# Modulation moved from the first attention (TensorE products) to the second (VectorE sums), context norm moved and done token by token

## The reference

```python
mod = jax.nn.silu(c) @ w_ada[l] + b_ada[l]
mod_c = jax.nn.silu(c_ctx) @ w_ada[l] + b_ada[l]
sh1, sc1, g1, sh2, sc2, g2 = jnp.split(mod[:, None, :], 6, axis=-1)
sh1c, sc1c, g1c, sh2c, sc2c, g2c = jnp.split(mod_c, 6)
mixed = _mixer(_modulate(ctx, sh1c, sc1c), _modulate(x, sh1, sc1), rows, w_in[l], ...)
```

## Time and profile before

| | |
|---|---|
| runs, us | 3023.42, 3021.66, 3011.48 (median 3021.66) |
| the profiled execution | 3016.62, its span 3014.8 |
| busy share of the span | PE 94%, PEld 76%, DVE 61%, ACT 42%, POOL 26% |
| chain that ended last, largest shares | PE 13%, DMA 4%, DVE 4% |
| DMA | 440.91 MB, mean 146 GB/s |

### The profile page before, as it was taken

One profiled execution on the slowest core, in us unless ns is written; L12 is line 12 of the kernel. 1 busy time (PEld: TensorE's weight loads), 2 busy tenths in 40 slices (PEclk: granted clock), 3 DMA queues, 4 the chain that ended last, 5 costly groups with the idle time before them and its releaser, 6 DMA issues. The chain is left out here.

```text
span 3014.8 us, 54412 instructions
## 1 busy us (share of the span) xinstructions
PE 2834.1 (94%) x22525; PEld 2295.6 (76%) x22525; DVE 1838.3 (61%) x2584; ACT 1272.0 (42%) x1629; POOL 796.9 (26%) x427
## 2 busy tenths in 40 slices
PE   9889999999999999999999999878989799999994
PEld 7467888889777777888867887567885478888883
DVE  3757663210343445655237967766656699999997
ACT  3544332222333334333226331423332277777775
POOL 2013444434333312444420000010000125544431
PEclk9999999999999999999999999889999799999997
DMA  4632422232211112222222200231003499999996
GB/s 173 236 142 112 98 97 98 98 131 96 84 58 69 71 57 84 98 97 97 98 99 98 84 23 12 102 142 46 32 18 124 161 333 363 370 372 368 379 368 260
DMA packets 83394, 440.91 MB, mean 146 GB/s; under 512 B 19712, under 2 KB 22784, under 8 KB 34816
## 3 DMA queue, kind: packets, MB, share of 16 engines
q1 hardware_dynamic: 73920, 429.63, 38.9%
q0 software_dynamic: 9280, 8.43, 0.8%
HBM read 423.30 MB, written 37.77 MB: 153 GB/s over the span
## 5 line engine op out<-in xcount | busy, mean ns | idle before, releaser
L85 POOL TENSOR_TENSOR ring_lo<-ring,unit_hi 128x2048 fp32r<-128x2048 f32 x110 | 507.3, 4612 | 1034.4 <-ACT unit_hi L74 1034.4
L146 PE MATMUL wide<-h_hi,unit_hi 128*128 128x512 f32 x1296 | 516.1, 398 | 11.7 <-DVE h_lo L623 5.0
L148 PE MATMUL wide<-h_hi,ring_lo 128*128 128x512 f32 x1296 | 507.0, 391 | 0.0
L147 PE MATMUL wide<-h_lo,unit_hi 128*128 128x512 f32 x1296 | 506.2, 391 | 0.0
L3479 DVE TENSOR_TENSOR ex_w_lo<-ring,ex_w_hi 128x2048 fp32r<-128x2048 f32 x194 | 442.1, 2290 | 41.6 <-ACT ex_w_hi L3474 40.8
L3474 ACT CAST ex_w_hi<-ring 128x2048 fp32r<-128x2048 f32 x194 | 369.5, 1908 | 111.5 <-DMA ring<-in_weights 99.3
L74 ACT CAST unit_hi<-ring 128x2048 fp32r<-128x2048 f32 x114 | 217.6, 1908 | 375.0 <-PE wide L148 370.8
L146 PEld LDWEIGHTS wide<-h_hi,unit_hi 128*128 128x128 f32 x1296 | 244.0, 188 | 71.4 <-issue 11.3
L148 PEld LDWEIGHTS wide<-h_hi,ring_lo 128*128 128x128 f32 x1296 | 244.1, 188 | 52.2
L147 PEld LDWEIGHTS wide<-h_lo,unit_hi 128*128 128x128 f32 x1296 | 244.4, 189 | 49.2 <-issue 0.7
L431 DVE TENSOR_TENSOR ffn_hidden_lo<-ffn_whole,ffn_hidden_hi 128x512 f32 (+1 forms) x44 | 201.3, 4575 | 51.9 <-ACT ffn_hidden_hi L402 51.9
(11 more groups left out here) (573 smaller groups left out, 5686.1 us busy)
## 6 DMA issues: line engine op xcount, KB each, us to landing
ring<-in_weights SPq DMA_DIRECT2D x356, 1024.0 KB, 6.2
rw_F<-factors SPq DMA_DIRECT2D x9, 1024.0 KB, 5.9
factors<-rp_out SPq DMA_DIRECT2D x4, 1280.0 KB, 5.3
factors<-rp_out SPq DMA_DIRECT2D x4, 1024.0 KB, 4.8
ex_both<-pair_rows_out SPq DMA_DIRECT2D x4, 1024.0 KB, 7.9
x<-in_x SPq DMA_DIRECT2D x8, 256.0 KB, 7.1
x_kept<-x SPq DMA_DIRECT2D x1, 2048.0 KB, 14.3
x<-x_kept SPq DMA_DIRECT2D x1, 2048.0 KB, 7.8
```

The source lines that it names most:

```text
L85: pool.tensor_tensor(self.lo[n % RING][:, :], self.ring[n % RING][:, :], self.hi[n % 2][:, :].bitcast(F32), ALU.subtract).then_inc(self.lo ...
L146: pe.matmul(dst, a[0], b[0], start=start, stop=False)
L147: pe.matmul(dst, a[0], b[1], start=False, stop=False)
L148: return pe.matmul(dst, a[1], b[0], start=False, stop=stop)
```

## The change

**Modulation.** It leaves attention A and the ring. `w_ada` is stored transposed, [48 x 128 outputs, 1024], and attention B computes each output as a sum along a row: one `tensor_tensor_reduce` on VectorE multiplies a chunk of 128 outputs x 512 inputs with half a row of silu(c) that stands in all partitions, and adds it up. There are 128 such sums (48 + 48 for `c`, 16 + 16 for `c_ctx`), each with a load of its own (256 KB) into one of two buffers; SyncE issues a load when the sum before last has released the buffer. silu of the conditions is taken in `v_b` on ScalarE, stored to HBM and loaded again spread over the partitions. Ring loads in attention B are now issued by ScalarE behind `write_hi` (`refill`), since SyncE's list holds the modulation's loads. The sums stand in VectorE's list: two behind each copy of a chunk of pair 0 but the first, then 6 in an item with two chunks and 3 in one with one chunk. `finish` (six small operations) stands in item 30.

**Context norm.** It moves from `out_a` to `out_b`, and works on tokens: two loads (512 KB each), `bn_stats`/`bn_aggr` on VectorE, a root on ScalarE, one normalising operation per 128 tokens, then four groups of four transposes on TensorE, after output chunks 1, 2, 3 and 5, whose results ScalarE scales, shifts and splits. Stores of the parts go to `out_b`, the four small stores of `mod_rows` from feed-forward 0 to 1.

```diff
@@ Weights
+    def refill(self, sp, i):
+        n = self.at + i
+        sp.wait_ge(self.used, n + 1)
+        sp.dma_start(self.ring[n % RING][:, :], self.stream[n + RING]).then_inc(self.loaded[n % RING], 16)
@@ ContextNorm
+    def moments(self, dve):
+        dve.wait_ge(self.loaded, 16 * (CTX // P))
+        for j in range(CTX // P):
+            for i in range(2):
+                dve.bn_stats(self.parts_of[:, j, i, :], self.rows[:, j, i * T:(i + 1) * T]).then_inc(self.step, 1)
...
+    def normalise(self, dve):
...
+        for j in range(CTX // P):
+            dve.tensor_scalar(self.rows[:, j, :], self.rows[:, j, :], self.stats[:, j, 0:1], self.rstd[:, j:j + 1],
+                              ALU.subtract, ALU.mult).then_inc(self.normed, 1)
...
+    def turn(self, pe, n):
+        if n == 0:
+            pe.wait_ge(self.normed, CTX // P)
+        else:
+            pe.wait_ge(self.placed, 2 * n)
...
@@ out_stage
+                if context:
+                    context.load(sp)
...
-                    context.square(act)
+                    context.root(act)
                 w.write_hi(act, 0, 2)
+                if context:
+                    context.place(act, 0)
+                    context.place(act, 1)
                 w.write_hi(act, 0, 3)
...
+                    if context and m_ in (3, 6):
+                        context.place(act, m_ // 3 + 1)
...
-                    if context and m_ == 0:
-                        context.tensor_sums(pe)
-                    if context and m_ == 3:
-                        context.tensor_squares(pe)
+                    if context and m_ in (1, 2, 3, 5):
+                        context.turn(pe, (1, 2, 3, 5).index(m_))
...
+                    if context and m_ in (0, 1, 4, 6):
+                        context.low(dve, (0, 1, 4, 6).index(m_))
@@ Modulation
+    DEEP, WIDE = 2, D // 2
...
+        for n, (f, m) in enumerate(self.steps):
+            if n >= self.DEEP:
+                sp.wait_ge(self.summed, n - self.DEEP + 1)
+            sp.dma_start(self.chunk[:, n % self.DEEP, :], self.ada[m, :, f % 2 * self.WIDE:(f % 2 + 1) * self.WIDE]).then_inc(self.loaded[n % self.DEEP], 16)
...
+    def vector(self, dve, n):
+        f, m = self.steps[n]
+        if m == 0:
+            dve.wait_ge(self.row_loaded[f % 2], 16 * (f // 2 + 1))
+        dve.wait_ge(self.loaded[n % self.DEEP], 16 * (n // self.DEEP + 1))
+        chunk, to = self.chunk[:, n % self.DEEP, :], (self.mod if f < 2 else self.mod1)
+        dve.tensor_tensor_reduce(chunk, chunk, self.rows[f % 2][:, :], 1.0, 0.0, ALU.mult, ALU.add, to[:, m, f % 2:f % 2 + 1]).then_inc(self.summed, 1)
@@ attention_stage, TensorE
-                    if modulation:
-                        for n in modulation.units_at(i, N):
-                            modulation.tensor(pe, n)
...
-                if modulation:
-                    modulation.add_strips(pe)
@@ attention_stage, VectorE
                 for j in range(per):
                     project.copy(dve, w, 0, j, pair_chunk_done, pair_chunk_copied)
+                    if j >= 1:
+                        sums(2)
...
+                    if chunks:
+                        sums(1)
...
+                    if len(chunks) == 1:
+                        sums(1)
...
+                        sums(2)
...
+                    if chunks:
+                        sums(1)
...
+                    if len(chunks) == 2:
+                        sums(2)
+                    if modulation and i == N - 2:
+                        assert next(summed, None) is None
+                        modulation.finish(dve)
@@ attention_stage, ScalarE
+                def write_hi(n):
+                    w.write_hi(act, 0, n)
+                    if n >= 2:
+                        w.refill(act, n - 2)
@@ values_b_stage
+                modulation.load_cond(sp, cond)
                 w.feed(sp, U_V_B)
+                modulation.store_cond(sp, cond)
...
                 normed.root(act)
+                modulation.silu(act, cond)
```

More of the change, by code:

```diff
@@ L492, in center @@
[L492 to L501, removed]
+        sp.dma_start(self.kept[1], self.parts[1][:, :, :].bitcast(F32)).then_inc(self.stored, 16)
@@ L509, in low @@
-    def low(self, dve):
-        for k in range(DC):
+        for j in range(CTX // P):
+            dve.tensor_scalar(self.rows[:, j, :], self.rows[:, j, :], self.stats[:, j, 0:1], self.rstd[:, j:j + 1],
[5 more added lines that the diff above has]
+            pe.wait_ge(self.placed, 2 * n)
+        for k in (2 * n, 2 * n + 1):
+            for j in range(CTX // P):
+                at = k % 2 * CTX + j * P
+                m = pe.transpose(self.c.bank[7][:, at:at + P], self.rows[:, j, k * P:(k + 1) * P], self.c.ident[:, :])
+        m.then_inc(self.turned, 1)
@@ new lines, in place, with low @@
+    def place(self, act, n):
+        act.wait_ge(self.turned, n + 1)
+        for k in (2 * n, 2 * n + 1):
+            act.activation(self.src[:, k, :], self.c.bank[7][:, k % 2 * CTX:(k % 2 + 1) * CTX], ACT.Identity,
+                           bias=self.shift(k), scale=self.scale(k)).then_inc(self.placed, 1)
+        for k in (2 * n, 2 * n + 1):
+            act.wait_ge(self.placed, k + 1)
+            act.copy(self.parts[0][:, k, :], self.src[:, k, :]).then_inc(self.hi_ready, 1)
+    def low(self, dve, n):
+        for k in (2 * n, 2 * n + 1):
@@ L523, in place @@
[L523 to L528, removed]
-        self.high(act, DC - 1)
-    def high(self, act, k):
-        act.wait_ge(self.placed, k + 1)
-        act.copy(self.parts[0][:, k, :], self.src[:, k, :]).then_inc(self.hi_ready, 1)
@@ L767, in sb, with load_cond, silu, store_cond @@
+    def load_cond(self, sp, room):
+        sp.dma_start(room, self.cond).then_inc(self.cond_loaded, 16)
+    def silu(self, act, room):
+        act.wait_ge(self.cond_loaded, 16)
+        act.activation(room, room, ACT.Silu).then_inc(self.cond_ready, 1)
+    def store_cond(self, sp, room):
+        sp.wait_ge(self.cond_ready, 1)
+        sp.dma_start(self.kept, room).then_inc(self.cond_stored, 16)
+    def place(self, ctx, nc):
         def sb(n, shape):
             return ctx.enter_context(nc.sbuf_tensor(f"ada_{n}", shape, F32))
-        self.c, self.w, self.cond, self.bias, self.mod, self.mod1 = c, w, cond, bias, mod, mod1
@@ L784, in tensor @@
-    def tensor(self, pe, n):
-        if n == 0:
-            pe.wait_ge(self.spread_ready, 1)
-        if n % 2 == 0 and n >= 2:
-            pe.wait_ge(self.rows_turned, n // 2)
-        unit = self.w.arrived(pe, 0, n)
-        for q in range(ADA_TILES):
-            m = pe.matmul(self.c.bank[7][q * ADA_WIDE:(q + 1) * ADA_WIDE, :], self.spread[:, n % 2 * ADA_TILES + q, :], unit[:, q * T:(q + 1) * T],
-                          start=(n % 2 == 0), stop=(n % 2 == 1))
-        m.then_inc(self.w.used, 1)
@@ L903, in _ @@
                 def _(sp):
-                    w.feed(sp, U_ADA)
+                    modulation.load(sp)
             if project:
@@ L1095, in _ @@
                                 write_due(due)
-    w.end(project.units if project else U_ADA, 1)
+                if project:
+                    for n in range(project.units - 2, project.units):
+                        w.refill(act, n)
+    w.end(project.units if project else 0, 1)
 def slopes():
```

205 lines of the change are left out of this document (90 added, 115 removed).

## The result

The changed kernel takes 3057.85 us (median of 3050.89, 3053.97, 3061.74 and 3061.88), the kernel before 3020.81 in the same comparison. The ratio is 1.0118, interval 1.0101 to 1.0135: slower by 1.2%, where 2999 us, 0.7% faster, was forecast. It is outside the range and on the side of rival C. Of all times in this document, two single executions in a slow state (8019 us with one sum behind the copy, 11772 us of the kernel before) are left out.

The account below looks back on a forecast made before the run. TensorE bounds attention B and both output projections; attention A is a loop over three engines. Terms -16.3, -1.0, -0.4, +4.3, +0.3, -8.5, +2.3 sum to -19.3 from 3016.62, giving 2997.3; median put at 2999, range 2988 to 3020.

Parts of the forecast that it names:

- rival C: Attention B: 256 KB loads land in 3.45 us or more, TensorE waits at second copies; at 3.5, net +17, 3035; chance 0.11.
- 17.7 with the start: Attention A: saving forecast from first negtop to ScalarE's first cast of out_a, including the start; 17.7 us.
- rival D: Attention A gives less: the other loop is nearer, or the clock falls (another 2 us); net -10, about 3009; chance 0.11.
- -1.0 at the start: Start of attention A: silu and the change of table no longer stand between negtop and the exponential; -1.0 us.
- -8.5: Output projection out_a: loses the context norm, falling from 60.25 to about out_b's 51.73; -8.5 us.
- +2.3: Output projection out_b: transposes, a low part on VectorE and a possible stall of the first group; +2.3 us, bounds 1.5 and 6.
- +0.3: Values of attention B (v_b): silu of the late-loaded conditions delays the cast and GpSimd's low part; +0.3 us, bounds 0 and 2.
- +4.3 for attention B: Attention B: cost of 128 sums on VectorE, start +3.7 and tail +0.6, steady state 0; bounds 0 and +25.
- rival B: Attention B: 256 KB loads land in 2.9 us, +13 over the item pairs; net -6, about 3012; chance 0.20.
- the replay: Attention B: VectorE's list replayed; beyond 2.55 us each 0.1 of landing costs 0.3 in some 13 item pairs.
- +3.7 before item 3: Start of attention B: three sums with two load waits between copies, +1.45 for items 0 and 1, +2.2 for item 2.
- 0.45 to 0.5 us: Attention B: room left for the next chunk copy behind the last sum, which waits for its load; 0.45 to 0.5 us.

Follow-up runs that it names:

- one sum behind the copy: The change with one sum per item moved on VectorE from ahead of the last chunk copy to behind it; 3035.72 us, ratio 1.0045.
- three-buffer kernel: The change with three chunk buffers instead of two and one row buffer given up, so half rows are reloaded; 3010.70 us, ratio 0.9973.
- half loads: The change with each load after the first two bringing 256 of 512 columns; attention B 363.9 us; total 4791.29 us, second block had other work.
- tiny sums: The change with all 128 loads kept but each sum working on only 8 of 512 columns; 3011.11 us, ratio 0.9964.
- without loads: The change with only the first two modulation loads made and all 128 sums kept, reading the first chunk; 3002.14 us, ratio 0.9933.

## Why the prediction was wrong

**What bounds the kernel.** Right. TensorE bounds attention B, and what delayed it was lost at once.

**Attention A.** Right, a little too large. From the first `negtop` to ScalarE's cast the change saved 13.4 us, and 15.7 in the three-buffer kernel, against 17.7 with the start. Its clock was at half rate for two stretches in the profiled execution of the change (0.92 granted) and 0.98 in the other; rival D's second half was thus real, and the difference between the two executions is about 2 us. The other limit was the one named in the earlier trace rows: TensorE's waits for the transposed probabilities rose from 9.8 to 17.0 us, and are 31 in place of 17.

```profile
PE wide L960 <- ACT att_a_probT L1108: 17.0, 31, 1.7
```

The -1.0 at the start came: the exponential now begins 0.2 us behind the start of `negtop` (85.25 and 85.05), 1.23 in the earlier trace rows.

**Context norm and `v_b`.** Right: -8.2 against -8.5, +2.5 against +2.3, 0 against +0.3. The first group of turns did not stall: the rows were normalised 11.3 us after the start of `out_b`, where 12 to 12.5 was estimated.

**The step that failed** is the landing in the term of +4.3 for attention B: "A load of 256 KB takes 2.4 us from issue to landing, 2.9 behind another". The row of 2.4 was of four loads of another stage. Here the landing was 2.88 without and 4.44 with a ring load, so even the better class was past the 2.55 that the prediction itself had worked out. That was rival B's number and more; with 47 of 128 loads at 4.4 it is rival C, given 0.11. The three buffers show that the wait is the cause. The step behind it, "In the steady state the cost is 0 while loads land within about 2.55 us", stood: with half loads, median 2.46, six groups of four items lost nothing. It is a bound on landing plus sum, though: with tiny sums they lost nothing at 3.0 either.

**What the replay lacked** is how delays add. It priced a landing by 0.3 us for each 0.1 over 2.55, once in a pair of items, which for 2.97 gives 16 and not the 38.7 of the six groups. The loss came in one item of four, not of two, and was 7 to 8 us each time. Two costs were missing, both in the rows at hand: a sum that slips into GpSimd's low part lasts 3.5 us (the prediction had this from the earlier trace rows, but only for sums that begin there by plan), and with each of the six stalls of over 5 us the clock went to its lower level for 3.4 to 6.8 us, beginning 0.5 to 3.7 us before the stall ended. The Trainium skill, "VectorE: DVE Perf Modes", section Two Vector instructions with no wait between them, and "GPSIMD Engine Reference", section Specifications, tells that VectorE and GpSimd share an SBUF interface when an instruction has two SBUF inputs; the sums' 0.69 and 3.52 us agree.

**The start** was right in kind and too small. The forecast had +3.7 before item 3, since no values step covers the waits there. The first four items lost 10.0 us in the change, 9.5 with half loads, 7.9 with tiny sums, 0.5 with three buffers and nothing without loads. The missing part is the same as above: in item 1 a sum waited 3.2 us for its load, lasted 3.2 beside GpSimd, and TensorE stood for 7.5.

**The size of a sum** was right: 0.65 against 0.69. So was that their number is no limit: without loads they cost nothing.

**Rival C's mechanism** was the one that came: its cause (a ring load under way), its wait (TensorE for the copy of a chunk behind a sum that waits for its load) and its sign. The place was another: not the second copy in an item with two, but the one copy of the item behind it, for which the forecast had left 0.45 to 0.5 us. Its price, 36 at 3.5 us, is near the 38.7 measured by luck, since there were half as many stalls, each dearer, at a median landing of 2.97. How the 49 divide between load, GpSimd and clock rests on the account of one trace above, since none of the three was taken away alone; two row buffers beside three chunk buffers, which would need no reloads, were not tried for want of SBUF.

## What to carry to other kernels

Where a transfer is issued by the end of the work that frees its buffer, its landing and that work add up, and the margin must be checked against the landing beside the largest other transfer of the stage, not against the best row. When a margin of 0.15 us (a landing of 2.4 against a limit of 2.55) carries the sum, price what lies beyond it in full: what the late instruction will meet next on the other engines, and the clock behind a stall. Cut a long stage at its period before reading a cause from its total: here 10 us of the loss were the start's, and two experiments left just these. A third buffer was worth 43 us here, a new order of the same work at most 16.

## What was not expected of the hardware

A 256 KB load landed in 2.88 us in the median with no ring load under way and 4.44 with one, on another queue; half the size in 2.36 and 3.62. The Trainium skill, "Trainium Kernel Development and Optimization", section Key Constraints, says that DMAs issued from the SP, ACT and POOL queues run on the same 16 engines and interleave; these numbers agree. A sum of 128x512 with two SBUF inputs took 0.69 us alone and up to 4.5 beside GpSimd's 4.6 us subtraction (4.9 in another kernel). It waits rather than being slowed: all 13 long sums of the change ended 0.55 us behind the end of that operation, whether they began 0.6 or 1.9 us into it, and sums of 8 columns took 3.0 to 3.3 us in that place. With each idle stretch of over 5 us of TensorE in attention B the granted clock went to its lower level for 3.4 to 6.8 us, beginning 0.5 to 3.7 us before the stretch ended.
